# Block 2's modulation vector as VectorE row sums in block 1's up projection, and block 2's head turned by feature tile

## What is computed

```python
c_act = jax.nn.silu(c)                       # c: (1, 1024)
for l in range(2):
    mod = c_act @ w_ada[l] + b_ada[l]        # w_ada[l]: (1024, 6144)
    sh_m, sc_m, gt_m, sh_f, sc_f, gt_f = jnp.split(mod, 6, axis=-1)
    h = rms_norm(x, g_mix[l]) * (1.0 + sc_m[:, None]) + sh_m[:, None]
    z = h @ w_in[l] + b_in[l]                # q, k, v, index and gate columns
    ...                                      # sparse attention, band attention, two gates
    x = x + gt_m[:, None] * (merged @ w_out[l])
    h2 = rms_norm(x, g_ffn[l]) * (1.0 + sc_f[:, None]) + sh_f[:, None]
    ...                                      # gate/up and down projections
    x = x + gt_f[:, None] * ffn
```

## Time and profile before

| | |
|---|---|
| median of 3 runs | 4503.64 us (4496.9 to 4510.25) |
| profiled execution, its own time | 4502.43 us |
| its span | 4500.6 us |
| mean granted TensorE clock | 0.937 of full speed |
| TensorE matmul busy | 4071.0 us, 90% of the span |
| VectorE, ScalarE, GpSimd busy | 1462.2, 1447.4, 1382.6 us (32%, 32%, 31%) |
| DMA | 357.88 MB, of it 329.26 MB on the weight ring's queue |

### The profile page before, as it was taken

How to read it: one execution, slowest core, us unless ns; L and a number is a source line. 1 busy time by engine, 2 the same in 40 slices (tenths; PEclk the granted TensorE clock), 3 DMA queues, 4 the chain that set the end, 5 groups by cost and what they waited for, 6 DMA issues and landing times.

```text
span 4500.6 us, 67045 instructions
## 1 busy us (share of the span) xinstructions
PE 4071.0 (90%) x28912; PEld 3195.5 (71%) x28912; DVE 1462.2 (32%) x2700; ACT 1447.4 (32%) x2491; POOL 1382.6 (31%) x583
## 2 busy tenths in 40 slices
PE   7898889999988987899899698998999698998999
PEld 5687568777866875688778475676887465686887
DVE  4443341411144533413211356214111274213112
ACT  3343152223223441522222322433222332433222
POOL 4000314444430003244444142123444141133443
PEclk9899899999988997999999798899999796999999
DMA  3001112232210002122222323222222323122222
GB/s 127 2 3 40 59 61 94 75 114 94 94 65 11 3 8 87 47 94 94 98 94 94 140 75 115 91 73 91 94 94 94 130 86 140 48 94 75 94 94 94
DMA packets 26926, 357.88 MB, mean 80 GB/s; under 512 B 3216, under 2 KB 3344, under 8 KB 4368
## 3 DMA queue, kind: packets, MB, share of 16 engines
q1 hardware_dynamic: 23040, 329.26, 19.8%
q10 hardware_dynamic: 3600, 24.37, 1.4%
HBM read 351.52 MB, written 2.10 MB: 79 GB/s over the span
## 4 chain that ended last, share of the span: by engine, by line
PE 80%; DVE 11%; ACT 4%; issue 2%; DMA 2%; POOL 1%; ACTq 0%; SPq 0%; DVEq 0%; PEldq 0%; POOLq 0%; PEld 0%
PE bank L658 20%; PE bank L659 20%; PE bank L660 20%; PE bank L987 11%; PE bank L1936 5%; ACT arena L2095 2%; DMA ring<-stream 1%; PE bank L1962 1%; DVE arena L2389 1%; PE bank L2040 1%; DVE arena L2388 1%; ACT arena L1317 1%; DVE arena L1733 1%; DVE arena L1636 1%; POOL ring_r L746 1%
## 5 line engine op out<-in xcount | busy, mean ns | idle before, releaser
L746 POOL TENSOR_TENSOR ring_r<-ring,hi_ring 128x1024 fp32r<-128x1024 f32 (+1 forms) x522 | 1269.0, 2435 | 2613.8 <-ACT hi_ring L737 2613.7
L658 PE MATMUL bank<-xT_r,ring_r 128*128 128x512 f32 x2288 | 917.9, 401 | 23.5 <-DVE x_lo_r L2457 17.3
L659 PE MATMUL bank<-x_lo_r,hi_ring 128*128 128x512 f32 x2288 | 910.1, 398 | 0.0
L660 PE MATMUL bank<-xT_r,hi_ring 128*128 128x512 f32 x2288 | 906.4, 396 | 0.0
L737 ACT ACTIVATE hi_ring<-ring 128x1024 fp32r<-128x1024 f32 (+1 forms) x522 | 542.9, 1046 | 670.8 <-PE bank L660 358.6
L658 PEld LDWEIGHTS bank<-xT_r,ring_r 128*128 128x128 f32 x2288 | 438.8, 192 | 132.1 <-issue 31.0
L660 PEld LDWEIGHTS bank<-xT_r,hi_ring 128*128 128x128 f32 x2288 | 436.3, 191 | 102.3
L659 PEld LDWEIGHTS bank<-x_lo_r,hi_ring 128*128 128x128 f32 x2288 | 437.8, 191 | 97.4 <-issue 2.1
L987 PE MATMUL bank<-arena 64*64 64x64 f32 (+4 forms) x7456 | 395.3, 249 | 78.2 <-DVE arena L1636 29.6
L1317 ACT ACTIVATE arena<-bank 128x512 f32<-128x512 f32 (+1 forms) x422 | 230.6, 548 | 686.2 <-PE bank L660 479.4
L987 PEld LDWEIGHTS bank<-arena 64*64 64x64 f32 (+2 forms) x7456 | 305.2, 140 | 135.0 <-issue 92.1
(11 more groups left out here) (244 smaller groups left out, 4953.0 us busy)
## 6 DMA issues: line engine op xcount, KB each, us to landing
ring<-stream SPq DMA_DIRECT2D x156, 2048.0 KB, 7.7
arena<-ln_rows ACTq DMA_DIRECT2D x5, 1024.0 KB, 8.0
arena<-edge ACTq DMA_DIRECT2D x4, 1024.0 KB, 6.5
arena<-edge ACTq DMA_DIRECT2D x2, 1792.0 KB, 7.5
arena<-pack ACTq DMA_DIRECT2D x2, 1540.0 KB, 7.5
arena<-pack ACTq DMA_DIRECT2D x2, 1200.5 KB, 14.4
x<-x_in SPq DMA_DIRECT2D x4, 512.0 KB, 7.4
arena<-pack ACTq DMA_DIRECT2D x2, 1024.0 KB, 6.5
```

What stands on the lines that cost most here:

```text
L658: first = nc.tensor.matmul(out_, left[1], right[0], start=start, stop=False)
L659: low = nc.tensor.matmul(out_, left[0], right[1], start=False, stop=False)
L660: return first, low, nc.tensor.matmul(out_, left[0], right[0], start=False, stop=stop)
L746: nc.gpsimd.tensor_tensor(feed.raw(n, ring_r), feed.raw(n), feed.hi(n).bitcast(F32), ALU.subtract).then_inc(split_lo, 1)
```

## The change

- `w_ada` is no longer among the ring's units (43 become 31 in each layer of block 2). It lies transposed in a tensor `ada`: 48 chunks of 128x1024 f32 (512 KB) for each layer, one for each 128 outputs. The vector `c` comes replicated to 128 partitions.
- In block 1, layer l, a new step `mod_open` ahead of `up 0` loads `c` and the first four chunks from ScalarE's queue, waits for `c`, and makes silu of it on ScalarE and VectorE. Then 48 steps `mod j` are spread between `up 2` and `up 31`: one VectorE multiply with row sum over 1024 columns, which leaves 128 elements of the modulation as a column. 18 of the 30 tiles get two of them and 12 get one. ScalarE issues the load of chunk j + 3 at step `mod j`, after it has waited for the sum before.
- `next 0` moves from before the up projection to behind it, and its load waits for the last row sum. The first `hid_split` waits for it on ScalarE too, since the chunks' buffers lie where the pairs go.
- `params` of block 2 adds the bias and makes both gains (five small VectorE operations).
- The tail ahead of block 2 gets splits 0 to 2 and `rms` of tiles 0 to 2 at `next 2`, and `rms` of tile 3 at the new `next 3`. In block 2's own tail these are new marks behind `store 2` and `store 3`.
- The head's `turn2` becomes `turn_d`, eight steps by feature tile: 4 transposes into a bank, one eviction of 128x512 on ScalarE that rounds, and on VectorE the same value at full precision and the subtraction. `rows qa i` waits for feature tiles up to 2i + 1 alone.
- In `attend(0)` the modulations are gone. At n = 3, 5, 7 and 14 a step `gt` spreads a quarter of the two gates: a VectorE copy of 128x512, 4 transposes, an eviction. The split of piece 24 (gates of the next stage) may come from n = 3 on, where it came from n = 27 on.

```diff
@@ steps_first @@
-    add("next", 0)
+    add("mod_open")
+    chunk = 0
     for i in range(FT1):
         if i == 8 and layer == 0:
             add("setup")
         add("up", i, banks=(2 + i % 2,))
+        while i >= 2 and chunk < min(MODS, MODS * (i - 1) // (FT1 - 2)):
+            add("mod", chunk)
+            chunk += 1
+    add("next", 0)
     down_steps(add, FT1)
     add("next", 1)
...
     add("norm_b", 1, 3)
+    add("next", 3)
@@ apart @@
-    early = [[("pack_load", ())], [("params", ())], [("split", (p,)) for p in range(AHEAD if k < L else 0)]] if k else []
+    early = [[("pack_load", ())], [("params", ())], [("split", (p,)) for p in range(AHEAD)], []] if k else []
+    if k >= L:
+        early[2] += [("rms", (0, tt)) for tt in range(TT - 1)]
+        early[3] += [("rms", (0, TT - 1))]
@@ steps_second @@
-    add("mod_row", 0, banks=(2,))
-    for k in range(4):
-        if k < 3:
-            add("mod_row", k + 1, banks=(2 + (k + 1) % 2,))
-        add("mod_c", k, banks=(4 + k % 2,))
-    for tt in range(TT):
-        add("turn2", 0, tt, banks=((0, 1), (6, 7))[tt % 2])
+    for d in range(DT):
+        add("turn_d", d, banks=((0, 1, 2, 3)[d % 4],))
...
-            if a == 0 and n % 4 == 3 and n < 28:
-                modulate(5 + n // 4, (1,))
+            if a == 0 and n in (3, 5, 7, 14):
+                add("gt", (3, 5, 7, 14).index(n), banks=(1,))
...
         add("store", tt)
+        if tt >= 2:
+            add("next", tt)
-    return number(with_splits(out, second_pieces(), {24: ("mod_g", 11), GU_PIECE: ("turn2", 1, 2)}))
+    return number(with_splits(out, second_pieces(), {24: ("gt", 0), GU_PIECE: ("turn2", 1, 2)}))
@@ first_scalar @@
+            elif name == "mod_open":
...
+                act.dma_start(c_rep, c_in).then_inc(c_loaded, 16)
+                for n_ in range(MOD_SLOTS):
+                    load_chunk(act, layer, n_)
+                act.wait_ge(c_loaded, 16)
+                f(c_half, c_rep, ACT.Tanh, scale=0.5).then_inc(c_tanh, 1)
+            elif name == "mod" and 0 < args[0] <= MODS - MOD_SLOTS:
+                act.wait_ge(mod_done, args[0])
+                load_chunk(act, layer, args[0] - 1 + MOD_SLOTS)
...
+                if name == "hid_split" and args[0] == 0:
+                    act.wait_ge(mod_done, MODS)
@@ first_vector @@
+            elif name == "mod":
+                j = args[0]
+                dve.wait_ge(mod_loaded[j % MOD_SLOTS], 16 * (j // MOD_SLOTS + 1))
+                V.tensor_tensor_reduce(out=mod_slot[j % MOD_SLOTS], in0=mod_slot[j % MOD_SLOTS], in1=c_rep, scale=1.0, scalar=0.0,
+                                       op0=ALU.mult, op1=ALU.add, accum_out=mod_of[layer][:, j:j + 1]).then_inc(mod_done, 1)
@@ second_tensor @@
+            elif name == "turn_d":
+                d = args[0]
                 take(b, n)
...
+                pe.wait_ge(xn_ready, TT)
+                for tt in range(TT):
+                    ins = nc.tensor.transpose(bank[b][:, tt * P:(tt + 1) * P], xn[0][:, tt, d * P:(d + 1) * P], C("ident"))
+                ins.then_inc(bank_full[b], 1)
...
-                if proj == "qa" and i == 0:
-                    drained(pe, uses, "turn2", 0, TT - 1)
+                if proj == "qa":
+                    drained(pe, uses, "turn_d", 2 * i + 1)
@@ second_scalar @@
+            elif name == "turn_d":
...
+                f(x_pair[0][:, d, :], bank[b][:, :], ACT.Identity, bias=mod_of[layer][:, d:d + 1],
+                  scale=gain[:, d:d + 1]).then_inc(turned_hi, 1)
@@ second_vector @@
+            elif name == "turn_d":
+                d = args[0]
+                dve.wait_ge(turned_hi, d + 1)
+                link(V.tensor_scalar(x_lo_value[:, d, :], bank[b][:, :], gain[:, d:d + 1], mod_of[layer][:, d:d + 1], ALU.mult, ALU.add))
+                V.tensor_tensor(x_pair[1][:, d, :], x_lo_value[:, d, :], x_pair[0][:, d, :].bitcast(F32), ALU.subtract)\
+                    .then_inc(bank_free[b], 1)
```

More of the change, by code:

```diff
@@ L120, in constants @@
     put("ident2", np.vstack([np.eye(CH)] * 2))
-    put("pick", np.ones((1, P)) * (np.arange(P) % 32 == 0)[:, None])
     put("ones_head", np.kron(np.eye(2), np.ones((CH, CH))))
@@ L426, in steps_second @@
     add("opened")
-    add("pack_rest")
     for tt in range(TT):
@@ L1476, in first_scalar, with load_chunk @@
         return step
+    def load_chunk(act, layer, j):
+        at_ = (layer * MODS + j) * P
+        act.dma_start(mod_slot[j % MOD_SLOTS], ada[at_:at_ + P, :]).then_inc(mod_loaded[j % MOD_SLOTS], 16)
     def first_gpsimd(pool, k_, layer, uses):
@@ L1527, in step @@
                 setup_vector(dve, link)
+            elif name == "mod_open":
+                dve.wait_ge(c_tanh, 1)
+                link(V.scalar_tensor_tensor(out=c_rep, in0=c_half, scalar=1.0, in1=c_rep, op0=ALU.add, op1=ALU.mult))
+                link(V.tensor_scalar(c_rep, c_rep, 0.5, None, ALU.mult))
+            elif name == "mod":
[3 more added lines that the diff above has]
+                                       op0=ALU.mult, op1=ALU.add, accum_out=mod_of[layer][:, j:j + 1]).then_inc(mod_done, 1)
             elif name == "params":
@@ L1867, in build @@
     half_bg = tiny(16)
-    mod = tiny(32)
+    mod_of = [tiny(MODS) for _ in range(L)]
     gain = tiny(16)
@@ L1873, in build @@
     gain_qb = tiny(64)
-    mod_ready = sem("mod_ready")
+    mod_loaded = [sem(f"mod{n}_loaded") for n in range(MOD_SLOTS)]
+    mod_done = sem("mod_done")
+    c_loaded = sem("c_loaded")
+    gt_ready = sem("gt_ready")
+    params2_ready = sem("params2_ready")
     square_done = sem("square_done")
@@ L1914, in setup_vector @@
         V = nc.vector
-        dve.wait_ge(c_tanh, 1)
-        link(V.scalar_tensor_tensor(out=c_col, in0=turns[:, 0:DT], scalar=1.0, in1=c_col, op0=ALU.add, op1=ALU.mult))
-        link(V.tensor_scalar(c_col, c_col, 0.5, None, ALU.mult))
+        dve.wait_ge(aux_loaded, 16)
         link(V.tensor_copy(pos_f, pos_i[:, :]))
@@ L1945, in begin @@
             feed.wait_loaded(pe, n)
-            return n > 0 and n - 1 not in MOD_UNITS
+            return n > 0
         def step(name, *args):
@@ L2267, in step @@
                 link(V.tensor_scalar(gain_qb, K2("qn_b"), 0.125, None, ALU.mult))
[L2268 to L2286 removed]
+                link(V.tensor_tensor(mod_of[layer], mod_of[layer], K2("b_mod"), ALU.add))
+                for at_ in range(2):
+                    cell = gain[:, 8 * at_:8 * at_ + 8]
+                    link(V.tensor_scalar(cell, mod_of[layer][:, 24 * at_ + 8:24 * at_ + 16], 1.0, None, ALU.add))
+                    ins = V.tensor_tensor(cell, cell, K2(("g_mix", "g_ffn")[at_]), ALU.mult)
+                    link(ins)
+                V.drain().then_inc(params2_ready, 1)
             elif name == "rms":
@@ L2445, in step @@
                 dve.wait_ge(x_added, at_)
+                drained(dve, uses, "gt", 2 * which + half)
                 filled(b_, n_)
@@ L2619, in second_units @@
 def second_units(i, l):
-    ada, w = i["w_ada_2"][l], i["w_in_2"][l]
-    ada = [unit_rows(ada[:, 512 * n:512 * n + 512], 512) for n in range(12)]
-    out = ada[0:4]
+    w = i["w_in_2"][l]
+    out = []
     out.append(unit_rows(w[:, 0:512], 512))
@@ L2685 @@
         "pos": i["positions_2"].reshape(TT, P).T,
-        "c_in": columns_of(i["c_2"].reshape(-1)),
+        "c_in": np.repeat(i["c_2"].reshape(1, D), P, axis=0),
+        "ada": np.concatenate([i["w_ada_2"][l].T for l in range(L)]),
     }
```

161 lines of the change are left out of this document (59 added, 102 removed).

## The result

The changed kernel takes 4431.69 us (4428.5 to 4436.38, 4 runs) against 4506.94 us (4496.9 to 4515.48, 4 runs) of the kernel before: ratio 0.9835, 95% interval 0.9811 to 0.9858, so 75 us or 1.65% less. A second comparison on one chip gave 4442.29 against 4504.33 us, ratio 0.9858 (0.9831 to 0.9886). The forecast was 4461 in 4408 to 4482. So the gain is 62 to 75 us by the two comparisons. The profiled execution took 4436.38, its span 4434.6: 66 us under that of before. It is the slowest of its four (4.7 over their median), and the one of before, 4502.43, lies 4.5 under the median of its kernel, so by stages there are 66 us to account for, not 75.

The account below looks back on a forecast made before the run. It took TensorE, busy 90% of the span, as the bound, losing time when standing still or at the slow clock. From 4502.4, -70.8 + 0 + 11.6 + 17.6 = -41.6 gave 4460.8, taken as 4461 us, range 4408 to 4482.

Parts of the forecast that it names:

- the forecast's own range: Range of the main case alone, without rivals, by the bounds of the head and up stage: 4445 to 4475 us.
- rival 1: First attention: the clock rises without the modulations, so +24 goes; 4437 if in one layer, 4413 in both; chance 0.25.
- The bound: Whole kernel: TensorE is busy 90% of the span; time is lost where it stands still or runs at the slow clock.
- The head: Block 2's two heads: modulation rows, sums and a wait for two units go; 34.0 and 36.8 us earlier, together -70.8.
- The sums: Up projection: 48 row sums a layer at 1.36 us each, hidden under TensorE, 5.27 of 5.52 a tile; cost 0.
- Rival 2: Up projection: sums and splits take turns until GpSimd is late, 7.47 us against 5.52 a tile; +70, 4531; chance 0.08.
- Up to down: Turn into the down projection: first hid_split waits for sum 48, stop 5.7 instead of 2.21; +5.8 a layer, +11.6 in all.
- attend(0): First attention: modulations go, early splits and gate transposes come, clock stays slow; +8.8 a layer, +17.6 (-30 to +30).
- the short rises: First attention, 2752 to 2827: attention products behind a modulation's rows lose the fast clock and take twice as long; +6.1 a layer.
- doubling: Last query tile of the first attention: 24 us at clock 1.00 take 48 without the modulation's rows; +24 a layer.
- The sum: All terms together: -41.6 us on the profiled execution's 4502.4, giving 4460.8, taken as 4461.

Follow-up runs that it names:

- the burst at n = 23: Changed kernel plus 16 dummy products of the removed modulation's form ahead of the transposes at n = 23 of each first attention; 4410.19 us, ratio 0.9796.
- the burst in a wait: Changed kernel with splits 24 to 26 from n = 24 and 16 dummy 128x512 products in the wait for the second gate quarter; 4411.76 us, ratio 0.98.
- all together: Changed kernel with splits 24 to 26 from n = 24, sums done by tile 29, 16 dummy products each at n = 5 and 17; 4355.87 us, ratio 0.967.

## Why the prediction was right, and where it was off

- **The number.** 4431.69 is inside the stated range of 4408 to 4482, but that is in part luck. It is outside the forecast's own range of 4445 to 4475, and nearest to 4437, which is rival 1 in one layer, while the trace shows that rival 1 did not come. The room that was left for rival 1 covers gains that came from elsewhere.
- **The bound.** Right: time was where TensorE stood at the heads, and ran slow in the attention. The change moved the total mostly through the first; the experiments did through both.
- **The head.** -70.8 forecast, -75.1 measured with the clock behind it (-73.2 without, which is what the forecast had summed: 35.8 and 37.4). The chain came in the order forecast: splits, squares, a normalisation of 6.4 us where laid end to end it had been priced like that, copies, turn. I didn't ask what each part was worth, though, and would have said the tail's work mattered; the kernel without it shows that it is worth 0 to 2.3 us a head, since the splits take back in the normalisation what they give ahead of the projection.
- **The sums.** Priced at 1.36, they are 1.22 alone and 1.56 by the group's mean. The cost of 0 held. The margin was thin by my sum (5.27 of 5.52), and the kernel with twice the work shows what lies past it. Rival 2 was to begin at a sum of 1.52 with its waits; at a mean of 1.56 no tile slipped. That mean counts time in which a split ran, and the 2.40 of the split was in the sum already.
- **Up to down.** +5.8 forecast, +5.4 and +5.8 measured; the stop forecast at 5.7 was 5.28 and 5.72. The kernel with earlier sums shows that this wait was nearly all of it: against the kernel before, its steps are +1.6 and 0.0.
- **Rival 1, the clock by itself.** It did not come in either layer: 126 us at 0.50, up to 7 us before the end. The prediction's reading that the rows bring the clock up was right, but its evidence was weaker than it said: in 3796 to 3830 it saw the attention's own products alone, and the rows of n = 19 stand there too (3805.35) without a rise. The Trainium skill's rule ("TensorE: Matmul & The Clock Gate", Part 1: The HAM clock gate) that activity releases the throttle fits if activity means more than being busy: the clock stayed at 0.50 with TensorE busy for 95.00 of 95 us, and rose within the dense burst.
- **attend(0).** The step that was mis-sized. Forecast +8.8 a layer (+9.5 behind the stop at its start), measured +4.0 and +1.0. In the first layer by parts: from the first head to n = 7, +6.0 forecast (the splits 4.7, two `gt` 1.3) and +9.3 measured (17.0 to 26.3 us), since the copy waited too; from there to the end of n = 23's modulation, -16.8 forecast (five modulations -25.5, two `gt` +2.6, the short rises +6.1) and -19.7 measured (72.9 to 53.2); behind it, +20.3 forecast (+24, less the last modulation's 3.7) and +14.4 measured (31.0 to 45.5). Net of the last modulation the stretch grew by 18.1, not by the 24 that doubling gave. Most of what is missing is that the clock rose near the end. The stretch after, in two parts:

```profile
2808.70:2847.00 38.30, 38.30 (x128) 26.74 (x128) 6.94 (x24) 11.69 (x27) 0.00 (x0) 0.50 0.00 1
2847.00:2854.20 7.20, 5.09 (x43) 4.44 (x41) 2.21 (x13) 3.65 (x8) 0.00 (x0) 0.97 0.10 22
```

  At 1.2 GHz the 5.09 busy us of the second part would be up to 5 more, an estimate that brings the 18.1 to 23; the last us are waits, which the clock doesn't stretch.
- **What was not forecast.** The second attention starts 5 us sooner in each layer: in the kernel before, the clock fell there for 10.2 us (from 2888.4 and from 3874.8), in the changed one for 3.4 at the stop. I can't say that the change caused it: a 10.2 us slow stretch is there again in one layer each of three of the kernels above, with the burst at n = 23 (from 3782.8), with the burst in a wait (from 3791.2) and with all together (from 2825.6). So 10.9 of the 66 us have no shown cause.
- **The sum.** -41.6 forecast for the profiled execution, -66 measured: 12.6 us from the first attentions, 4.3 from the heads, 10.9 from the second attentions, 0.4 from the turns into the down projection and 2.5 from where nothing changed, less 5.8 between heads and attentions. The median moved by 75; against it the forecast of 43 was short by 32, of which 9 is that the profiled executions lie 4.7 over and 4.5 under the medians of their kernels. Against the second comparison, 62 us, it was short by 19.

## What to carry to other kernels

When a piece of dense TensorE work is moved to an idle engine, look at what its clock was worth to the work behind it: one burst of 4.57 us at n = 23 gave 13 us a layer more than it cost. Sparse but busy stretches that run at 1.2 GHz can be worth a burst of dummy products behind each stop (two bursts a layer and two moved edges gave 86 us here). And price work on GpSimd by what VectorE does at the same time: three splits moved into a quiet-looking place cost TensorE 6 us, and moving them in the tail behind the last square, into the head, gave nothing.

## What the runs showed of the hardware that I had not expected

- TensorE at 1.2 GHz for 95 us while busy for 95.00 of them, and for 51.00 of 51 in another run: a busy column says nothing of the clock.
- A stop of TensorE of 1.53 or 1.54 us, with one of 0.76 ahead of it, was followed within 1 us by a fall of the clock from 2.4 GHz, in both layers of two kernels, after heads had kept it for 17 to 20 us. That the stop caused it is likely and not shown alone.
- The same rows of a modulation raised the clock eleven times and left it at 1.2 GHz once, and behind eight of the rises it fell again within 4 us.
- A copy on VectorE with one input took 2.56 us beside a GpSimd split instead of 0.42, and four scaled copies started only when three splits behind one another were over.
